# Half-size (Strassen) products for the last item of an expert in a mixture-of-experts encoder, with the weight sums on VectorE

## The reference, cut to what matters

```python
def expert_block(args):                     # 128 rows of one expert
    e, tok, gt = args
    xb = hf[tok]
    g = xb @ w_gate[e] + b_gate[e]
    u = xb @ w_up[e] + b_up[e]
    g = jnp.minimum(g, SWIGLU_LIMIT)
    u = jnp.clip(u, -SWIGLU_LIMIT, SWIGLU_LIMIT)
    act = (u + 1.0) * (g * jax.nn.sigmoid(g * SWIGLU_ALPHA))
    y = act @ w_down[e] + b_down[e]
    return y * gt[:, None].astype(y.dtype)
```

## Time and profile before

| | |
|---|---|
| median of 3 runs | 2185.58 us (2183.75 to 2186.74) |
| profiled execution, span | 2183.0 us |
| around the span, against the median | 2.6 us |
| TensorE busy, matmuls | 2114.3 us, 97% |
| VectorE busy | 701.9 us, 32% |
| ScalarE busy | 620.8 us, 28% |
| GpSimd busy | 525.2 us, 24% |
| mean granted TensorE clock | 0.986 |
| moved by DMA | 485 MB, 222 GB/s mean |

### The profile page before, as it was taken

The page is one execution under the profiler, slowest core; times in us unless marked ns, Lnnn a source line. Parts: engine busy times, 40 slices in busy tenths (PEclk is TensorE's granted clock), DMA queues, the critical chain, the costliest instruction groups (busy, mean ns, idle before and its releaser), DMA issues.

```text
span 2183.0 us, 30745 instructions
## 1 busy us (share of the span) xinstructions
PE 2114.3 (97%) x10224; PEld 997.9 (46%) x10225; DVE 701.9 (32%) x1953; ACT 620.8 (28%) x1206; POOL 525.2 (24%) x537
## 2 busy tenths in 40 slices
PE   8999999996999999999998999999999999999997
PEld 6547676443444444344343434434443444444443
DVE  4322998674221222212222231222122311222123
ACT  2000887122222332222222222221222222232223
POOL 3181124133111221211122122211212121222223
PEclk9999999997999999999999999999999999999998
DMA  8001100237668678578859686675889867666774
GB/s 309 9 35 47 73 1 1 69 111 305 250 225 299 221 255 321 183 257 320 331 172 391 226 286 244 233 276 181 324 307 373 309 248 289 216 252 251 250 253 186
DMA packets 151899, 485.04 MB, mean 222 GB/s; under 512 B 20288, under 2 KB 37973, under 8 KB 151310
## 3 DMA queue, kind: packets, MB, share of 16 engines
q1 hardware_dynamic: 116192, 444.81, 52.9%
q0 software_dynamic: 33792, 34.66, 7.6%
q10 hardware_dynamic: 1874, 5.02, 0.6%
HBM read 461.26 MB, written 43.09 MB: 231 GB/s over the span
## 4 chain that ended last, share of the span: by engine, by line
PE 94%; DMA 3%; POOL 1%; issue 1%; DVE 1%; ACT 0%; ACTq 0%; SPq 0%; POOLq 0%; DVEq 0%
PE psum L1903 43%; PE psum L1938 15%; PE psum L1542 7%; PE psum L1949 5%; PE psum L1648 4%; PE psum L1681 3%; PE psum L1641 3%; PE psum L1538 2%; PE psum L1829 2%; PE psum L1890 2%; PE psum L1911 2%; DMA weights<-in_w_down 2%; PE psum L1961 1%; PE psum L1973 1%; PE psum L1690 1%; DMA weights<-in_w_up 1%
## 5 line engine op out<-in xcount | busy, mean ns | idle before, releaser
L1903 PE MATMUL psum<-weights,work 128*128 128x512 f32 (+2 forms) x3008 | 949.7, 595 | 1.9 <-DMA weights<-in_w_up 1.9
L1903 PEld LDWEIGHTS psum<-weights,work 128*128 128x128 f32 (+2 forms) x3008 | 366.5, 159 | 516.7 <-issue 515.3
L766 POOL DMA_INDIRECT residual_rows<-work x184 | 287.2, 1561 | 531.6 <-ACT work L999 481.5
L1938 PE MATMUL psum<-weights,work 128*128 128x512 f32 x768 | 337.5, 592 | 0.0
L1350 DVE SCALAR_TENSOR_TENSOR work<-psum,work 128x4 f32<-128x4 f32 x47 | 7.6, 162 | 838.0 <-PE psum L1822 838.0
L723 POOL DMA_INDIRECT work<-normed_rows,work x47 | 53.2, 1132 | 742.1 <-PE psum L1829 575.9
L1938 PEld LDWEIGHTS psum<-weights,work 128*128 128x128 f32 x768 | 142.2, 190 | 160.7 <-issue 160.7
L969 ACT ACTIVATE work<-psum 128x256 f32<-128x256 f32 x188 | 71.9, 382 | 418.6 <-PE psum L1903 391.7
L1418 DVE TENSOR_SCALAR work<-psum 128x256 f32<-128x256 f32 x188 | 79.7, 424 | 290.3 <-ACT work L969 289.8
L999 ACT ACTIVATE work<-psum,work 128x256 f32<-128x256 f32 x184 | 72.1, 475 | 319.3 <-PE psum L1938 229.5
L949 ACT ACTIVATE work<-psum 128x512 f32<-128x512 f32 x96 | 57.6, 600 | 345.0 <-PE psum L1829 344.5
(11 more groups left out here) (257 smaller groups left out, 1906.4 us busy)
## 6 DMA issues: line engine op xcount, KB each, us to landing
weights<-in_w_gate SPq DMA_DIRECT2D x64, 2048.0 KB
weights<-in_w_up SPq DMA_DIRECT2D x64, 2048.0 KB
weights<-in_w_down SPq DMA_DIRECT2D x64, 2048.0 KB
residual_rows<-x SPq DMA_DIRECT2D x9, 512.0 KB, 2.8
normed_rows<-work ACTq DMA_DIRECT2D x9, 512.0 KB, 2.7
x<-in_x SPq DMA_DIRECT2D x8, 512.0 KB, 8.7
weights<-in_w_in SPq DMA_DIRECT2D x16, 256.0 KB, 8.9
weights<-in_w_in SPq DMA_DIRECT2D x8, 512.0 KB, 11.1
```

The lines of the kernel that those rows point to most:

```text
L766: pl.indirect_dma_start(acc_d[:, :], bass.IndirectOffsetOnAxis(dest[:, b:b + 1], 0), yrow[:, b * BLK:(b + 1) * BLK], None, bounds_check=UN ...
L1903: mm = pe.matmul(out.rearrange("p (m n) -> p m n", m=2), xT[:, k, lo:lo + cols], wgu[:, :, k, blk * BLK:(blk + 1) * BLK], start=(k == 0), ...
L1938: mm = pe.matmul(bank(4 + h), actT[:, k, :], wdn[:, k, h * HALF:(h + 1) * HALF], start=False, stop=(k == DT - 1))
```

## The change

In the last item of each expert but the last one:

- With more than 96 rows (`split_item`), gate and up are made from seven products of half size in each of three dimensions (64 rows, half of K, half of the columns) in the place of eight. They need four sums of tokens and four differences of weights (T1 = B12 - B11, T2 = B22 - T1, T3 = B22 - B12, T4 = B21 - T2), which VectorE makes in the rows that held `x`; then combinations of products that ScalarE keeps (`keep`) and VectorE adds.
- With 96 rows or fewer, TensorE's body is nearly the old one (`main=True`), with its units in other banks and the ends of all three units of a 96 ahead of the transposes. VectorE makes the same differences and combinations, with the kept ones times `on` = 0.
- VectorE's and ScalarE's loop over items becomes a loop over experts, in which `run_early` is a loop of seven passes with a condition for the early items, and then the body of the last item.
- The loads of the next weights wait for the differences too.
- The item tables get two more columns and entries; eight small VectorE operations are added to them.

The core of the diff (tables and renames left out):

```diff
             with sp.Fori(1, EXPERTS) as e:
-                done = sp.value_load(ends[0:1, bass.ds(e - 1, 1)], min_val=1, max_val=MAX_ITEMS)
-                sp.wait_ge(s_k03, done)
+                last = sp.value_load(lasts[0:1, bass.ds(e - 1, 1)], min_val=0, max_val=MAX_ITEMS - 2)
+                sp.wait_ge(s_k03, last + 1)
+                sp.wait_ge(s_wts, 8 * e + (WTS0 - 2))
                 for m in range(2):
                     load_gu(m, 0, bass.ds(e, 1))
-                sp.wait_ge(s_gu, UNIT * done)
+                sp.wait_ge(s_wts, 8 * e + WTS0)
+                sp.wait_ge(s_gu, UNIT * last + (UNIT - 1))
                 for m in range(2):
                     load_gu(m, 1, bass.ds(e, 1))
...
+            def keep(n, src, e):
+                act.wait_ge(s_prod, 3 * e + (n + 1))
+                act.activation(kept[:, n, :, :].rearrange("p m c -> p (m c)"), bank(src), ACT.Copy).then_inc(s_kept, 1)
...
+            with act.Fori(0, EXPERTS - 1) as e:
+                begin = act.value_load(ends[0:1, bass.ds(e, 1)], min_val=0, max_val=MAX_ITEMS - 1)
+                j = act.value_load(lasts[0:1, bass.ds(e, 1)], min_val=0, max_val=MAX_ITEMS - 2)
+                run_early(begin, j)
+                choose(j, e)
+                keep(0, 0, e)
+                keep(1, 1, e)
+                act.wait_ge(s_tok, 4 * e + (TOK0 + 4))
+                move_xT(j + 1, 0)
+                unit_sigmoid(j, e, 0)
+                unit_sigmoid(j, e, 1)
+                unit_sigmoid(j, e, 2)
+                unit_move_hidden(j, 0)
+                unit_move_hidden(j, 1)
+                unit_move_hidden(j, 2)
+                unit_sigmoid(j, e, 3)
+                move_xT(j + 1, 1)
+                unit_move_hidden(j, 3)
+                store_scaled(j)
...
+            def run_early(begin, end):
+                with dve.Fori(0, TT - 1) as n:
+                    with dve.If(begin + n < end):
+                        j = begin + n
...
+            def weight_sum(e, n, part):
+                ks = slice(2 * part, 2 * part + 2)
+                own = [wgt_half(0, 1), wgt_half(0, 0), wgt_half(1, 0), wgt_half(1, 1)]
+                b11, b12, b22, b21 = (w[:, :, ks, :] for w in own)
+                to, a, b = ((0, b12, b11), (1, b22, sums[:, 0, :, ks, :]), (0, b22, b12), (1, b21, sums[:, 1, :, ks, :]))[n]
+                dve.tensor_tensor(sums[:, to, :, ks, :], a, b, ALU.subtract).then_inc(s_wts, 1)
...
+            with dve.Fori(0, EXPERTS - 1) as e:
+                begin = dve.value_load(ends[0:1, bass.ds(e, 1)], min_val=0, max_val=MAX_ITEMS - 1)
+                j = dve.value_load(lasts[0:1, bass.ds(e, 1)], min_val=0, max_val=MAX_ITEMS - 2)
+                run_early(begin, j)
+                local, chain = item_chain(j)
+                e3 = dve.value_load(items[0:1, bass.ds(j + 3, 1)], min_val=0, max_val=EXPERTS - 1)
+                kind = dve.value_load(items[0:1, bass.ds(j + 2 * TABLE, 1)], min_val=0, max_val=KINDS - 1)
+                on = split[:, bass.ds(j, 1)]
+                dve.wait_ge(s_wk[0], 32 * e + 32)
+                weight_sum(e, 0, 0)
+                weight_sum(e, 0, 1)
+                dve.wait_ge(s_xT, 2 * j + 2)
+                token_sum(e, 0)
+                token_sum(e, 1)
...
+                token_sum(e, 2)
...
+                token_sum(e, 3)
+                dve.wait_ge(s_wk[1], 32 * e + 32)
+                dve.wait_ge(s_wts, 8 * e + (WTS0 + 2))
+                weight_sum(e, 1, 0)
+                weight_sum(e, 1, 1)
+                dve.wait_ge(s_prod, 3 * e + 2)
+                dve.wait_ge(s_wts, 8 * e + (WTS0 + 4))
+                weight_sum(e, 2, 0)
+                weight_sum(e, 2, 1)
+                dve.wait_ge(s_gu, UNIT * j + 1)
+                dve.wait_ge(s_kept, 2 * e + 1)
+                dve.scalar_tensor_tensor(halves[:, 0], kept[:, 0], on, unit_bank(0), ALU.mult, ALU.add).then_inc(s_u, 1)
+                find_places(j, chain, kind)
+                dve.wait_ge(s_prod, 3 * e + 3)
+                dve.tensor_tensor(kept[:, 2], first_bank, kept[:, 0], ALU.add).then_inc(s_u, 1)
...
+                dve.tensor_tensor(kept[:, 1], kept[:, 1], kept[:, 2], ALU.add).then_inc(s_u, 1)
+                weight_sum(e, 3, 0)
+                dve.wait_ge(s_gu, UNIT * j + 2)
...
+                dve.scalar_tensor_tensor(halves[:, 1], kept[:, 1], on, unit_bank(1), ALU.mult, ALU.add).then_inc(s_u, 1)
+                dve.tensor_tensor(kept[:, 0], unit_bank(1), kept[:, 2], ALU.add).then_inc(s_u, 1)
+                weight_sum(e, 3, 1)
+                gated(j, 0)
+                dve.wait_ge(s_gu, UNIT * j + 3)
+                dve.scalar_tensor_tensor(halves[:, 2], kept[:, 1], on, unit_bank(2), ALU.mult, ALU.add).then_inc(s_u, 1)
+                gated(j, 1)
+                next_seen(j)
+                next_row_numbers(j, chain)
+                gated(j, 2)
+                dve.wait_ge(s_gu, UNIT * j + 4)
...
+                dve.scalar_tensor_tensor(halves[:, 3], kept[:, 0], on, unit_bank(3), ALU.mult, ALU.add).then_inc(s_u, 1)
+                gated(j, 3)
+                find_third(j, chain, e3)
...
                 for b in range(units):
+                    if main and b == 2:
+                        pe.wait_ge(s_kept, 2 * e + 2)
                     mm = gate_up(b, range(4))
...
                 if tokens == 96:
                     gate_up_ends(0)
                     gate_up_ends(1)
+                    if main:
+                        gate_up_ends(2)
                     next_rows()
                     hidden(0)
-                    gate_up_ends(2)
+                    if not main:
+                        gate_up_ends(2)
...
+            def split_item(j, e, e2):
...
+                def product(to, tokens, weights, k, start, ends):
+                    for g in range(2):
+                        out = PS[64 * g:64 * g + 64, to * HALF:(to + 1) * HALF].rearrange("p (m n) -> p m n", m=2)
+                        mm = pe.matmul(out, tokens[:, k, :], weights[:, :, k, g * BLK:(g + 1) * BLK],
+                                       start=start and k == 0, stop=ends and k == 3)
+                    return mm
...
+                for k in range(4):
+                    mm = product(0, a11, wgt_half(0, 1), k, True, True)
+                mm.then_inc(s_prod, 1)
+
+                pe.wait_ge(s_tok, 4 * e + (TOK0 + 1))
+                summed(0, 1, s1, True, False).then_inc(s_k03, 1)
+                pe.wait_ge(s_chosen, j + 1)
+                bias(1, 0, True).then_inc(s_prod, 1)
...
+                row_transposes(0)
...
+                for k in range(4):
+                    product(3, a12, wgt_half(1, 1), k, True, False)
+                bias(3, 1, True).then_inc(s_gu, 1)
...
+                summed(1, 0, s2, True, True).then_inc(s_prod, 1)
...
+                summed(2, 2, s3, True, True).then_inc(s_gu, 1)
...
+                for k in range(4):
+                    mm = product(1, s4, wgt_half(1, 0), k, True, True)
+                mm.then_inc(s_gu, 1)
...
+                summed(3, 3, a22, True, False)
+                bias(3, 1, True).then_inc(s_gu, 1)
...
+                transposes(0)
+                transposes(1)
+                pe.wait_ge(s_seen, j + 1)
+                row_transposes(1)
+                transposes(2)
+                pe.wait_ge(s_wk[2], 16 * e + 16)
+                pe.wait_ge(s_aTm, UNIT * j + 4)
+                for k in range(4):
+                    mm = down(k)
+                mm.then_inc(s_d03, 1)
+                transposes(3)
+                pe.wait_ge(s_wk[3], 16 * e + 16)
+                pe.wait_ge(s_aTm, UNIT * j + 5)
+                for k in range(4, DT):
+                    mm = down(k)
+                mm.then_inc(s_dps, 1)
```

More of the change, by code:

```diff
@@ L180, in encoder_kernel @@
         gsum, ginv, iota_p, iota_t, missing, limits = (small(c) for c in (8, 8, 1, 1, 1, 7))
-        of_p, ofc, less = (small(c) for c in (4, 1, 1))
+        of_p, ofc, less, is_main = (small(c) for c in (COLUMNS, 1, 1, 1))
         iota_c = small(CHUNK)
@@ L200, in encoder_kernel @@
         items = small(3 * TABLE)[0:1, :].bitcast(I32)
-        ends = small(EXPERTS)[0:1, :].bitcast(I32)
+        ends = small(EXPERTS + 1)[0:1, :].bitcast(I32)
+        lasts = small(EXPERTS)[0:1, :].bitcast(I32)
         bounds = Z[:, 17536:17536 + 3 * TABLE]
-        last_of, first = bounds[:, 0:TABLE], bounds[:, 2 * TABLE:]
+        last_of, first, split = (bounds[:, n * TABLE:(n + 1) * TABLE] for n in range(3))
         total = small(2)[0:1, :].bitcast(I32)
@@ new lines, in item_chain, with chain, find_places @@
+            def item_chain(j):
+                local = [0]
+                def chain(ins):
+                    local[0] += 1
+                    ins.then_inc(s_dve, 1)
+                    dve.wait_ge(s_dve, j * PER + (LOOP0 + local[0]))
+                return local, chain
+            def find_places(j, chain, kind):
+                dve.wait_ge(s_ips, j + 3)
```

(5 more changed lines are left out.)

295 lines of the change are left out of this document (221 added, 74 removed).

## The result

The changed kernel takes **2442.59 us** (median of 4 runs, 2439.65 to 2446.15), the kernel before beside it 2186.16 (2183.75 to 2186.9): ratio **1.117**, 95% interval 1.116 to 1.119, 256 us slower. The forecast was 2380 with a range of 2270 to 2450. The profiled execution spans 2437.9 us, 254.9 more than before.

A forecast was written before the change was run, and what follows sets the result against it. TensorE was taken as the bound. Waits for late sums and bias rows, less saved products, summed to +172 us, plus 21 for clock: 193 over 2185.6, so 2380. Range 2270 to 2450, from rival (a) to rival (b)'s upper end plus hand-overs.

The forecast's parts named there:

- rival (b): Waits and passes: slow clock behind every long wait, 2 us each, passes of 0.85 us; 2410, or 2431 with longer differences; chance 0.17.
- What bounds the kernel: Whole kernel: TensorE, 94% of the chain that ended last, so its time counts in full if replacements are ready in time.
- Saved on TensorE: Products of 23 split items: 3.0 us less each, 1.3 left after what is added; 30 us in all.
- Differences: VectorE, 31 last items: eight differences each of 2.3 us (bounds 2.1 and 2.44), 18.4 us an item.
- Empty passes: Loops over early items: each empty pass costs VectorE 0.72 us and ScalarE 0.42, delaying first difference and bias rows.
- Rival (a): Loops over early items: empty passes cost nothing, as the sequencer works ahead under VectorE's last operation; 2273 us; chance 0.13.
- Split items: Split last items: 44.9 us on time, 52.8 after an early 32, 50.3 after an early 64; +10, +61, +31 in all.
- VectorE sets the pace: Split items, after product 4: VectorE's combinations, differences and hidden blocks, 12.6 us, set the length, not TensorE.
- Last 96s and 64s: Unsplit last items gain nothing and wait: +7.5 us for each of six 96s, +45; +1 and +21 around the 64s.
- Clock: TensorE behind 21 waits over 3.5 us: slower clock costs 0 to 2 us each, taken as 1; +21.
- Loads: Loads of the next weights, now also waiting for T3 and T4, 12.9 and 24 us into a split item: nothing late.

The follow-up runs named there:

- the kernel with one pass: Changed kernel with one pass instead of seven in VectorE's and ScalarE's loops over early items: 2342.03 us, ratio 1.073.
- the short differences: Changed kernel with each weight difference formed over 8 of its 256 columns, the rest left out (output not the reference's): 2342.04 us, ratio 1.074.
- my own variant: Changed kernel with sums in split items only, last items of 96 and 64 rows run as before the change, five TensorE bodies: 2447.64 us, ratio 1.121.
- four bodies: Kernel with all four edits and weights released early, but without the 96-row body; items of 65 to 96 rows run as full ones: 2228.17 us, ratio 1.019.
- in a row: Kernel with all four edits and weights released early, with the unsplit full body moved behind the other bodies: 2176.41 us, ratio 0.995.
- the kernel with copies covered: Changed kernel with TensorE's order at the end of a split item changed so that ScalarE's two copies have cover: 2426.57 us, ratio 1.112.

## Why the prediction was right, and where not

The direction and the main mechanism held: TensorE is the bound, and waits for late sums and late bias rows outweigh the saved products. The time was 62 us above the forecast, inside the range of 2270 to 2450 but above the forecast's own 2325 to 2425 and above both figures of rival (b), 2410 and 2431. That it is inside is partly luck: the range reached 2450 for other reasons, 48 us came from a term that I did not have, and the waits were 50 us fewer than I had them. By its own steps:

- **What bounds the kernel.** Right: TensorE, so each wait counts in full.
- **Saved on TensorE.** The products save 2.9 us an item (27.57 to 24.65), forecast 3.0. Given back are 2.8 and not 1.7: 0.8 for bias groups, 0.4 for the transposes of hidden blocks, 0.2 for the next rows', 0.3 for the down matmuls and the rest, and 1.1 for two stretches of 0.56 in which TensorE waits for ScalarE's copy of a transposed block (I had 1.2). No run shows the other 0.5 of my 1.7, which was my estimate for bias groups; in the changed kernel a pair of bias matmuls takes 0.40 us, 0.34 up to the next row (line 2295, 870.62 to 870.96), and an item has three such pairs. Net 0.15 us, not 1.3; in a kernel without late work an item takes 43.8 us against 44.0. This mis-sized term is the only gain the change had.
- **Differences.** Right: 2.29 us each, 248 rows, 559 us.
- **Empty passes.** Right, and shown by the kernel with one pass, 95 us. Rival (a) fell.
- **Split items.** The times were right (45.2 for 44.9; 53.5 to 54.1 for 52.8 and 1 of clock), the reason in part wrong. The waits before product 2 and for the bias (1.34 for 1.0) are as forecast, but behind them TensorE and not VectorE sets the pace, as the short differences showed. Two mistakes cancelled, the pace too long and the saving too large.
- **Last 96s and 64s.** In the 96s each wait is within 0.7 us. Two of the six take 45.2 and 45.3, 1 us over 35.7 + 7.5 + 1; the other four have a long branch besides.
- **Clock.** Mis-sized: 1 us a wait. Item 9 lost 1.9 (its products took 26.56 us, 24.65 in an item without the wait), and the 13 split items with a wait of 4 us or more lost 1.6 to 2.7 each. The kernel before has 2.0 behind its 7.2 us wait, and 1.4 behind its 3.15 us wait, worked out from 3.3 us at a granted clock of 0.57; rival (b) took 2. Of my grounds for halving it, one was false (VectorE sets the pace), and the other did not help: in item 9 the clock fell to 0.50 at 862.0, 3.3 us before the wait ended, and the loss was whole all the same. In each of the 13, all of them waits for VectorE, the granted clock read 0.50 at the end of the wait or just behind it, for 3.4 us (four), 6.8 us (eight) or 10.2 us (one). With long branches as a second source of stops, the records lost 57 us in all where I had 21.
- **Missing: the jumps.** 48 us of stops at branches, and part of the slow clock behind them, were in no term. The diff shows seven bodies for four; the trace of before had the queue's row and branches of 0.2 us, and I read neither as something that could change.
- **Loads.** Right for the changed kernel, none was late. But it was near: in my own variant a leave given at the end of a last 64 made TensorE wait 12.5 us.
- **GpSimd.** The scatters took 1.97 us instead of 1.56, and with short differences 1.57 again. The kernel before has a like pair: the same GpSimd operation took 0.40 us, and 1.48 where it began at 510.19 together with VectorE's comparison of 1.23 us (L1333). My sum had no term for this, and it needed none: no wait for a scatter shows on TensorE.

Net: waits 50 us fewer than forecast, 29 us less saved, 36 more for the clock, 48 for jumps, 63 together.

With the waits removed, the jumps placed well and the copies covered, the same Strassen products are worth about 1 us in each of 23 items (43.0 against 44.1), and the kernel is 0.6% faster than before.

What stays open: whether the price of a jump hangs on the distance to the target or on the total span of code in use (in every kernel here both went together), and how the last long branch, behind the last item (4.7 us), could go.

## What to carry to other kernels

A saving of 7% of an item's matmuls is small change: count what new groups, transposes and uncovered copies give back before anything else, then ask when the first sum is ready rather than how much summing there is. Where a runtime branch chooses between large bodies, count the instructions from the first body in use to the last, look at the instruction queue's row, and put rare bodies at the end (48 us here). A wait of 4 to 8 us cost TensorE its own length and then 1.6 to 2.7 us at a lower clock behind it; one of 1.3 us cost no more than itself (24.71 us of products against 24.65).

## What the runs showed of the hardware

**Jumps in TensorE's program.** Counting TensorE's records in one run of each body: full 291, split 406, 32 rows 488, 64 rows 284, 96 rows 567. From the first used body to the last this gives 1630 in the kernel before, 1469 with four bodies, 1745 in a row: no long branch in the loop, and 7, 6 and 11 instruction packets of 16 KB from the first item on. With the full body in between, which runs for the last item alone, it gives 2036 and the dispatch, and nearly 2800 or more in the kernels with seven bodies: 10 to 21 long branches in the loop, and 45 to 93 packets. So the long branches in the loop set in somewhere between 1745 and 2036 and the dispatch, an estimate from these counts alone. A long branch in the loop took 3.2 to 7.7 us here, though a packet itself took 1.0 us in the median (0.9 to 2.2).

**The granted clock behind a stop.** Behind a stop of 8.3 us it was 0.71 over the next 5.8 us, 0.50 in the first 3.4 of them, and 1.00 when the same stretch was filled with work. A stop of 2.9 us at a branch was enough to cost the next item's products 1.7 us (26.34 against 24.65), with the clock at 0.50 for 3.4 of them (1001.9 to 1005.3 in the changed kernel). In the kernel with copies covered the same item follows a stop of 2.8 us, the clock stays at 1.00, and its products took 24.64: the price of such a stop is not the same each time.
